# Delta rule steps with a doubled Gram buffer, their preparation moved ahead of the solve

## The chip, the core and the metric

The kernel runs on one core of a Trainium2 chip. The metric is the time on the device of one execution, in microseconds (us), as the median of several runs. The engines are named as in the profile: PE (TensorE matmuls) and PEld (its weight loads), DVE (VectorE), ACT (ScalarE), POOL (GpSimd) and SP (SyncE, which issues most DMAs).

## What is computed

The kernel is a whole two-block network on 256 tokens of width 1024, all in float32. The first block is attention, convolution and memory branches and a mixture of 32 experts. The second block reads the first block's output and a context of 256 tokens; it holds two recurrences, each in two directions: a state space one (SSD) and a gated delta rule (GDN). The change touches the delta rule only. The reference solves it in chunks (cut to what matters):

```python
def gdn_chunk_scan(q, k, v, log_a, beta, s0):
    """Gated delta rule S_t = a_t (I - b_t k_t k_t^T) S_{t-1} + b_t k_t v_t^T, o_t = S_t^T q_t, chunked"""
    g = jnp.cumsum(log_a, axis=2)
    diff = g[:, :, :, None] - g[:, :, None, :]
    a_mat = jnp.einsum("bclhd,bcshd->bclsh", k, k) * beta[:, :, :, None] * masked_exp(diff, strict)
    lhs = jnp.moveaxis(a_mat, -1, 2) + jnp.eye(CHUNK, dtype=a_mat.dtype)
    rhs = jnp.concatenate([v * beta[..., None], k * (beta * jnp.exp(g))[..., None]], -1)
    sol = lax.linalg.triangular_solve(lhs, ..., left_side=True, lower=True, unit_diagonal=True)
    ...
    def step(s, inp):
        v_new = u_c - jnp.einsum("bhlk,bhkv->bhlv", w_c, s)
        o = jnp.einsum("bhlk,bhkv->bhlv", qg_c, s) + jnp.einsum("bhls,bhsv->bhlv", qk_c, v_new)
        s = s * dec_c[..., None, None] + jnp.einsum("bhlk,bhlv->bhkv", kd_c, v_new)
```

## The kernel before, in words

The kernel uses chunks of 128 tokens and 8 heads. There are eight delta steps, m = 0 to 7 (`STEPS`: direction, index in the direction, chunk). Steps 0 to 3 go over the context; they are interleaved with the experts of the first block by a planner (`context_phases` gives each phase a cost, `mixed_schedule` spreads them between the expert phases). Steps 4 to 7 go over the latent tokens and stand behind the experts, with little else beside them.

Every engine runs its own program in order, and waits on semaphores. For the delta steps all four programs (`gdn_pe`, `gdn_act`, `gdn_dve`, `gdn_pool`) walk the same list of phases from `delta_phases`, and each does its own part of a phase. Phases in `STATE_FREE` don't need the state and are done for step m+1 while step m runs. The phases are:

- `rows`: PE turns the cumulated log decays into rows (tile gR), L2058; DVE subtracts and clips them out of PSUM into the matrices A and QK (L1258); ACT takes their exponentials (L1024 for A, L1028 for QK); POOL masks QK (L1624). PE also turns the keys (gkT), which ACT copies out to kT (L1013).
- `gram`: PE forms keys by keys (gKK, L630); DVE multiplies it into A (L1270), copies the diagonal blocks out (L1277, L1279, L1280) and spreads them (L1284).
- `rep`: PE replicates the spread blocks (gRep, L655), ACT copies them to `rep` (L1034); POOL masks A to its off-diagonal part (L1644) and inverts the 16 by 16 diagonal blocks by substitution (L1646, and 15 pairs of L1652 and L1653) into Y.
- `expand`: DVE expands Y to the block diagonal matrix XT (L1294).
- `kS`: PE multiplies keys by the state (gK), ACT scales it into T (L1043), POOL forms U = beta times v (L1633), DVE subtracts T = U - T (L1302).
- `M`, `u`, `M2`, `t`, `w`, `x`, `v`: the block solve. PE multiplies (L630), ACT copies out M, MT, U, M2T and T (L1013), DVE adds the products w, x and v into U (L1305). `M` needs XT. In `M2` POOL also forms k_rest (L1638).
- `cross`: keys by queries (DVE L1290). `out`: the output and the new state (DVE L1316, L1317, L1325, L1326).

PE works into PSUM banks 0 to 5 in turn (`open_tile`: a tile takes the next bank, and PE waits until that bank's last tile is drained). A tile of 4 heads fills a bank, so a phase takes two banks (`M` and `out` up to four). While the experts run, these are banks 0 to 4.

`second_block_pe`, `_act`, `_dve` and `_pool` put other work between the phases of steps 4 to 7: modulation products (PE L2211 and L821, DVE L1469) at the phases of `MOD_PHASES`, and on DVE `q_squares` (L1487) behind `M 4` and `M 5`, on which PE's `q_sums` (L828, behind `M2 4` and `M2 5`) wait; `normed_y` (L1483) behind `kS 6`, `u 6`, `M2 6` and `v 6`; POOL's gate gain (L1709) behind `u 5` and `u 6`.

Steps that use the same chunk as the step before (`SAME_KEYS`: steps 2 and 6) keep its kT.

Of the kernel before, what the change touches and what calls it, by code (L numbers as in the profile page):

```python
# [14 lines left out]
P = 128  # L15
# [6 lines left out]
STATE_FREE = ("rows", "gram", "rep", "cross", "expand")  # L22
# [89 lines left out]
def delta_phases(steps):  # L112

    order = [(phase, steps[0]) for phase in STATE_FREE]
    for m in steps:
        for phase in ("kS", "M", "rows", "u", "M2", "gram", "t", "w", "rep", "x", "v", "cross", "out", "expand"):
            if phase not in STATE_FREE:
                order.append((phase, m))
            elif m + 1 in steps:
                order.append((phase, m + 1))  # L120
    return order


def context_phases():

    delta = {"rows": 2.4, "gram": 2.0, "rep": 3.6, "kS": 1.9, "M": 3.8, "u": 1.9, "M2": 1.9, "t": 1.9, "w": 1.9, "x": 1.9,
# [57 lines left out]
def two_block_kernel(nc, a, out):  # L184
# [3 lines left out]
    with ctx:  # L188
# [26 lines left out]
        AREA = 35760  # L215
        area = sb("area", [P, AREA])

# [144 lines left out]
        def delta_buffers(wide, keys, triangle, MT_at, M2_at, U_at, T_at, K_at, QK_at, small_at):  # L362
            return {"spread": at(wide, 16, GDN_HEADS, 16), "rep": at(wide, 16, GDN_HEADS, 16), "XT": at(wide, GDN_HEADS, P),
                    "kT": at(keys, GDN_HEADS, P), "A": at(triangle, GDN_HEADS, P), "MT": at(MT_at, GDN_HEADS, P),
                    "M2T": at(M2_at, GDN_HEADS, P), "U": at(U_at, GDN_HEADS, P), "T": at(T_at, GDN_HEADS, P),
                    "M": at(K_at, GDN_HEADS, P), "k_rest": at(K_at, GDN_HEADS, P), "QK": [at(place, GDN_HEADS, P) for place in QK_at],
                    "rows": at(small_at, GDN_HEADS, 16), "Y": at(small_at + 128, 16, GDN_HEADS), "step": at(small_at + 256, 16, GDN_HEADS),
                    "pairs": at(small_at + 384, GDN_HEADS, 32)}
# [250 lines left out]
        def gdn_pe(pe, steps, open_tile, transposes):  # L619

            for phase, m in delta_phases(steps):
# [11 lines left out]
                def of(name):  # L633
                    return lambda head: b[name][:, head, :]

                if phase == "rows":
                    pe.wait_ge(s["kn_ready"], c + 1)
                    for h in range(0 if m in SAME_KEYS else 2):
                        transposes(("gkT", m, h), [k_gdn[side][:, t, head * P:(head + 1) * P] for head in range(4 * h, 4 * h + 4)])
                    for h in range(2):  # L640
                        transposes(("gR", m, h), [cum[side][:, d, t, 16 + head:17 + head].to_broadcast([P, P])
                                                  for head in range(4 * h, 4 * h + 4)])
# [93 lines left out]
        def second_block_pe(pe, open_tile, unit, used, transposes, product, tokens_by_weights, split_product):  # L736
# [33 lines left out]
            for i, m in enumerate(LATENT):  # L770
# [19 lines left out]
                if i == 3:  # L790
                    assert next(delta_steps) == "rows 4"
                    gate_tiles(GATES[6:7])
# [211 lines left out]
        def gdn_act(eng, steps):  # L1004

            for phase, m in delta_phases(steps):
# [8 lines left out]
                if phase == "rows":  # L1015
                    for h in range(0 if m in SAME_KEYS else 2):
                        out4("gkT", h, "kT")
                    for h in range(2):
                        part = b["A"][:, 4 * h:4 * h + 4, :]
# [64 lines left out]
        def second_block_act(eng, root, copy_out):  # L1084
# [14 lines left out]
            for i, m in enumerate(LATENT):  # L1099
# [3 lines left out]
                if i == 3:  # L1103
                    assert next(delta_steps) == "rows 4"
                for kind, half, t in GATES[2 * i:2 * i + 2]:
# [134 lines left out]
        def gdn_dve(eng, steps, link, spread):  # L1240

            v = nc.vector
            for phase, m in delta_phases(steps):
# [8 lines left out]
                if phase == "rows":  # L1252
                    for which, clip in (("A", ALU.max), ("QK", ALU.min))[:1 + side]:
                        dst = b["A"] if which == "A" else b["QK"][m % 2]
# [9 lines left out]
                if phase == "gram":  # L1264
                    for h, heads in halves:
                        eng.wait_ge(s["gdn_decay"], 2 * m + h + 1)
                        src = four("gKK", h)
                        for i in range(4):
                            head = 4 * h + i
                            ins = v.scalar_tensor_tensor(b["A"][:, head, :], src[:, i, :], beta[side][:, t, 8 * d + head:8 * d + head + 1],  # L1270
                                                         b["A"][:, head, :], ALU.mult, ALU.mult)
# [3 lines left out]
                    for q in range(4):  # L1275
                        part = slice(32 * q, 32 * q + 32)
                        ins = v.tensor_copy(b["pairs"][part, :, :], b["A"][part, :, part])  # L1277
# [3 lines left out]
                    if m not in (0, 4):  # L1281
                        wait_filled(eng, ("gu", m - 1, 1))
# [96 lines left out]
        def second_block_dve(eng, step, link, root_mean, root_ask, root_take, square_sums, spread):  # L1379
# [27 lines left out]
            for i, m in enumerate(LATENT):  # L1407
# [44 lines left out]
                if i == 3:  # L1452
                    assert next(delta_steps) == "rows 4"
                    assert next(delta_steps) == "gram 4"
# [155 lines left out]
        def gdn_pool(eng, g, steps, link):  # L1610

            for phase, m in delta_phases(steps):
# [27 lines left out]
                if phase == "rep":  # L1640
                    eng.wait_ge(s["spread_ready"], m + 1)
                    for h, heads, dims in halves:
                        part = b["A"][:, heads, :]
# [1250 lines left out]
```

## Time and profile before

| what | value |
|---|---|
| time, median of 3 runs | 1719.59 us (1716.0 to 1723.46) |
| profiled execution: span, first to last instruction | 1712.1 us |
| PE busy | 1554.9 us (91%) |
| PEld busy | 1062.7 us (62%) |
| DVE busy | 693.0 us (40%) |
| ACT busy | 375.5 us (22%) |
| POOL busy | 219.8 us (13%) |
| DMA | 372.53 MB, mean 218 GB/s |
| DMA busy in slices 12 to 22 of 40 | nine tenths or more, but one with seven |

The profiled execution has no time of its own beside its span; the median of the runs is 7.5 us above the span. The chain of work that ended last is PE for 70% of the span, DMA for 16%, DVE for 8%. The page's slices are 42.8 us each: slices 11 to 22 hold the experts and context (DMA at 400 GB/s), slices 29 to 32 the delta steps 4 to 7 (DMA at 50 to 150 GB/s, PE between seven and nine tenths busy). A row of the timeline gives the start, the time from the first to the last of a merged run of instructions, their engine, line, operation, tiles and count, and in brackets how long the engine was idle before it and what ended that.

### The profile page before, as it was taken

The numbers are of one execution on the slowest core, as the hardware profiler recorded it, in microseconds if no ns is written. First come the engines' busy times: TensorE is split into PE (matmuls) and PEld (weight loads), VectorE is DVE, ScalarE is ACT, GpSimd is POOL, SyncE is SP. The second block draws the span as 40 slices with busy tenths as digits, with TensorE's granted clock in tenths as the row PEclk, the third lists the DMA queues.
The fourth block names the chain that finished last, engine by engine and source line by source line (L and its number), as shares of the span: only waits on it lengthen the run. The fifth ranks groups of instructions, "written<-read, shape, count | busy, mean of one in ns | idle before, by whom it ended". The sixth has DMA issues, their size and how long they took to land.

```text
span 1712.1 us, 22993 instructions
## 1 busy us (share of the span) xinstructions
PE 1554.9 (91%) x9392; PEld 1062.7 (62%) x9392; DVE 693.0 (40%) x1459; ACT 375.5 (22%) x829; POOL 219.8 (13%) x368
## 2 busy tenths in 40 slices
PE   7999999999989797888998799999988799999996
PEld 3548655545766464456676478865577764788742
DVE  2206312434533343634443447776766750400003
ACT  1001245201411112232232132142333320100000
POOL 2000000002000000223313010001455512300000
PEclk9999999998999898899999999999999999999998
DMA  8444423564599999799999914442531144344430
GB/s 259 148 147 148 147 98 137 219 227 197 204 407 408 406 408 401 312 399 417 382 373 419 393 64 146 148 145 70 200 140 50 50 148 148 102 160 156 165 130 25
DMA packets 124286, 372.53 MB, mean 218 GB/s; under 512 B 10524, under 2 KB 26518, under 8 KB 107414
## 3 DMA queue, kind: packets, MB, share of 16 engines
q1 hardware_dynamic: 118245, 361.12, 55.8%
q0 software_dynamic: 1568, 8.39, 1.3%
q10 hardware_dynamic: 4368, 1.54, 0.4%
q8 instruction: 77, 1.26, 0.3%
q14 instruction: 28, 0.22, 0.0%
HBM read 369.98 MB, written 1.05 MB: 217 GB/s over the span
## 4 chain that ended last, share of the span: by engine, by line
PE 70%; DMA 16%; DVE 8%; ACT 2%; issue 1%; POOL 1%; SPq 0%; DVEq 0%; ACTq 0%; POOLq 0%
PE psum L2064 48%; PE psum L630 6%; DMA ring<-in_w_down 6%; DMA ring<-in_w_up 5%; PE psum L1859 4%; DMA area<-in_w_in 2%; PE psum L2058 2%; PE psum L1843 2%; PE psum L1900 1%; PE psum L1881 1%; PE psum L655 1%; DMA area<-in_w_down 1%; PE psum L2181 1%; DVE area L1294 1%; POOL area L1652 1%
## 5 line engine op out<-in xcount | busy, mean ns | idle before, releaser
L2064 PE MATMUL psum<-ring,area 128*128 128x512 f32 (+1 forms) x1040 | 448.9, 590 | 8.6 <-DMA ring<-in_w_proj_mem 2.1
L2064 PE MATMUL psum<-area,ring 128*128 128x256 f32 (+1 forms) x1920 | 412.1, 374 | 5.9 <-DMA ring<-in_w_in 4.3
L2064 PEld LDWEIGHTS psum<-area,ring 128*128 128x128 f32 x1920 | 352.8, 191 | 54.3 <-DMA ring<-in_w_in 5.4
L2064 PEld LDWEIGHTS psum<-ring,area 128*128 128x128 f32 x1040 | 196.9, 191 | 246.7 <-issue 243.4
L630 PE MATMUL psum<-area 128*128 128x128 f32 x1536 | 195.3, 286 | 20.7 <-DVE area L1294 17.5
L630 PEld LDWEIGHTS psum<-area 128*128 128x128 f32 x1536 | 185.8, 200 | 43.0 <-issue 19.0
L2337 ACT ACTIVATE area<-psum 128x512 f32<-128x512 f32 x116 | 66.0, 599 | 450.2 <-PE psum L2064 334.0
L1859 PE MATMUL psum<-ring,area 128*32 128x256 f32 x1728 | 111.9, 404 | 34.5 <-DMA ring<-in_w_up 34.4
L1859 PEld LDWEIGHTS psum<-ring,area 128*32 128x32 f32 x1728 | 57.9, 115 | 77.8 <-issue 51.8
L2058 PE MATMUL psum<-const,area 128*128 128x128 f32 x528 | 84.5, 286 | 20.6 <-DVE area L1387 4.8
L2058 PEld LDWEIGHTS psum<-const,area 128*128 128x128 f32 x528 | 65.0, 145 | 55.4 <-issue 24.4
L1210 DVE SCALAR_TENSOR_TENSOR area<-area,cols 128x268 f32<-128x268 f32 (+1 forms) x186 | 91.6, 492 | 6.6
L1601 POOL TENSOR_TENSOR area<-area 128x1024 f32<-128x1024 f32 x4 | 9.8, 2464 | 462.3 <-DVE area L2459 462.3
L1013 ACT COPY area<-psum 128x512 f32<-128x512 f32 x92 | 52.2, 586 | 68.6 <-PE psum L630 63.2
L1881 PE MATMUL psum<-ring,area 128*32 128x256 f32 x800 | 53.7, 399 | 14.4 <-DMA ring<-in_w_down 12.7
L976 ACT COPY area<-psum 128x256 f32<-128x256 f32 x62 | 23.1, 373 | 197.8 <-PE psum L2064 197.8
L1591 DVE TENSOR_TENSOR area<-psum,area 128x512 f32<-128x512 f32 x11 | 7.6, 691 | 140.7 <-PE psum L2064 140.7
L1208 DVE TENSOR_SCALAR area<-area,cols 128x268 f32<-128x268 f32 (+1 forms) x62 | 22.0, 356 | 104.4 <-ACT area L976 104.4
L2064 PE MATMUL psum<-area 128*128 128x256 f32 (+3 forms) x288 | 59.8, 361 | 3.9 <-DMA area<-in_w_in 2.9
L2064 PEld LDWEIGHTS psum<-area 128*128 128x128 f32 (+1 forms) x288 | 47.3, 199 | 14.2 <-issue 5.1
L1551 DVE TENSOR_TENSOR area<-psum,area 128x512 f32<-128x512 f32 x8 | 5.5, 686 | 114.5 <-PE psum L2064 114.5
L1652 POOL TENSOR_TENSOR area<-area 128x120 f32<-128x120 f32 (+14 forms) x120 | 44.9, 374 | 38.7 <-ACT area L1034 29.9
(318 smaller groups left out, 1407.6 us busy)
## 6 DMA issues: line engine op xcount, KB each, us to landing
ring<-in_w_in SPq DMA_DIRECT2D x29, 2048.0 KB, 8.3
ring<-in_w_gate SPq DMA_DIRECT2D x54, 1024.0 KB, 10.2
ring<-in_w_up SPq DMA_DIRECT2D x54, 1024.0 KB, 12.0
ring<-in_w_down SPq DMA_DIRECT2D x50, 1024.0 KB, 13.7
ring<-in_w_ada SPq DMA_DIRECT2D x12, 2048.0 KB, 8.7
area<-in_w_down SPq DMA_DIRECT2D x14, 1024.0 KB, 15.0
ring<-in_w_out SPq DMA_DIRECT2D x6, 2048.0 KB, 7.8
area<-in_w_gate SPq DMA_DIRECT2D x10, 1024.0 KB, 13.1
```

The costliest lines, as they stand in the source:

```text
L630: last = nc.tensor.matmul(dst[:, i * P:(i + 1) * P], lhs(4 * h + i), rhs(4 * h + i), start=True, stop=True)
L976: nc.scalar.copy(dst, src).then_inc(drain_of(key), 1)
L1013: nc.scalar.copy(b[name][:, 4 * h:4 * h + 4, :], src).then_inc(drain_of((key, m, h)), 1)
L1208: link(v.tensor_scalar(dst, src, w, None, ALU.mult))
L1210: link(v.scalar_tensor_tensor(dst, src, w, dst, ALU.mult, ALU.add))
L1652: link(g.tensor_tensor(tmp[:, 0:n, :], rep[:, left, :, j], Y[:, j:j + 1, :].to_broadcast([P, n, GDN_HEADS]), ALU.mult))
L1843: last = nc.tensor.matmul(dst[:, j * P:(j + 1) * P], h2[:, t, k * P:(k + 1) * P], place[:, t, q * P:(q + 1) * P], start=t == 0, stop=t == ...
L1859: last = nc.tensor.matmul(wide.dst[CAP * j:CAP * (j + 1), 0:2 * P], hcT[:, q % 2, k, rows], both[:, :, k % 4, j * P:(j + 1) * P], start=k ...
L1881: last = nc.tensor.matmul(dst[CAP * g:CAP * (g + 1), 0:256], actT_e[:, e % 2, CAP * j:CAP * (j + 1)], w[:, j % 2, g * 256:(g + 1) * 256], ...
L2058: last = nc.tensor.transpose(t[0:width, j * P:j * P + rows], src, ident[0:rows, 0:rows])
L2064: last = nc.tensor.matmul(dst, lhs(k), rhs(k), start=first and k == 0, stop=final and k == count - 1)
L2337: nc.scalar.activation(dst, src, func).then_inc(drain_of(key), 1)
```

## The change

The order of phases in a step becomes

```python
STATE_FREE = ("rows", "keys", "gram", "rep", "cross", "expand")
for phase in ("rows", "kS", "keys", "gram", "M", "u", "M2", "rep", "t", "w", "x", "v", "cross", "out", "expand"):
```

where rows, keys, gram, rep, cross and expand are those of step m+1. Before it was

```python
for phase in ("kS", "M", "rows", "u", "M2", "gram", "t", "w", "rep", "x", "v", "cross", "out", "expand"):
```

The old phase rows is cut in two. On PE, rows keeps the decay rows (gR) and keys has the turned keys (gkT). On ACT everything of it moves to keys: the copies of gkT and the exponentials of A and QK. On DVE the clips stay in rows, and on POOL the mask of QK stays in rows. A gets a second buffer (used by step parity), XT gets one of its own and no longer shares space with spread and rep, and DVE's wait for gu of the step before ahead of the spreading (L1284) is gone. For the space the reserve for descriptors of DMAs that POOL issues is set to 1024 bytes a partition, from its default, and the common area is cut by 300 elements.

```diff
@@ delta_phases, context_phases
-STATE_FREE = ("rows", "gram", "rep", "cross", "expand")
+STATE_FREE = ("rows", "keys", "gram", "rep", "cross", "expand")
...
-        for phase in ("kS", "M", "rows", "u", "M2", "gram", "t", "w", "rep", "x", "v", "cross", "out", "expand"):
+        for phase in ("rows", "kS", "keys", "gram", "M", "u", "M2", "rep", "t", "w", "x", "v", "cross", "out", "expand"):
...
-    delta = {"rows": 2.4, "gram": 2.0, "rep": 3.6, "kS": 1.9, "M": 3.8, "u": 1.9, "M2": 1.9, "t": 1.9, "w": 1.9, "x": 1.9,
+    delta = {"rows": 1.9, "keys": 0.5, "gram": 2.0, "rep": 3.6, "kS": 1.9, "M": 3.8, "u": 1.9, "M2": 1.9, "t": 1.9, "w": 1.9, "x": 1.9,
@@ buffers
-        AREA = 35760
+        AREA = 35460
         area = sb("area", [P, AREA])
+        delta_extra = sb("delta_extra", [P, 2, GDN_HEADS, P])
...
-            return {"spread": at(wide, 16, GDN_HEADS, 16), "rep": at(wide, 16, GDN_HEADS, 16), "XT": at(wide, GDN_HEADS, P),
-                    "kT": at(keys, GDN_HEADS, P), "A": at(triangle, GDN_HEADS, P), "MT": at(MT_at, GDN_HEADS, P),
+            return {"spread": at(wide, 16, GDN_HEADS, 16), "rep": at(wide, 16, GDN_HEADS, 16), "XT": delta_extra[:, 0, :, :],
+                    "kT": at(keys, GDN_HEADS, P), "A": [at(triangle, GDN_HEADS, P), delta_extra[:, 1, :, :]], "MT": at(MT_at, GDN_HEADS, P),
@@ gdn_pe
                 if phase == "rows":
+                    for h in range(2):
+                        transposes(("gR", m, h), [cum[side][:, d, t, 16 + head:17 + head].to_broadcast([P, P])
+                                                  for head in range(4 * h, 4 * h + 4)])
+                if phase == "keys":
                     pe.wait_ge(s["kn_ready"], c + 1)
                     for h in range(0 if m in SAME_KEYS else 2):
                         transposes(("gkT", m, h), [k_gdn[side][:, t, head * P:(head + 1) * P] for head in range(4 * h, 4 * h + 4)])
-                    for h in range(2):
-                        transposes(("gR", m, h), [cum[side][:, d, t, 16 + head:17 + head].to_broadcast([P, P])
-                                                  for head in range(4 * h, 4 * h + 4)])
@@ gdn_act
-                if phase == "rows":
+                if phase == "keys":
                     for h in range(0 if m in SAME_KEYS else 2):
                         out4("gkT", h, "kT")
@@ gdn_dve, phase gram
-                    if m not in (0, 4):
-                        wait_filled(eng, ("gu", m - 1, 1))
                     rows = b["rows"].rearrange("p h j -> p (h j)")
@@ kernel
-    nc = _bacc.Bacc("TRN2", target_bir_lowering=False, num_devices=1)
+    nc = _bacc.Bacc("TRN2", target_bir_lowering=False, num_devices=1, dynamic_dma_scratch_size=1024)
```

Elsewhere b["A"] becomes b["A"][m % 2], and `keys 4` is taken behind `rows 4` in PE's, ACT's and DVE's programs of the second block.

## Rows read from the trace of the kernel before

**Rows 1.** Windows of the expert stage: stretch, length, busy of each engine, clock, DMA share, GB/s
```profile
750.00:765.00 15.00, 15.00 (x156) 9.74 (x155) 5.63 (x14) 8.14 (x14) 0.00 (x0) 1.00 0.93 366
...
810.00:825.00 15.00, 15.00 (x141) 10.89 (x140) 5.82 (x14) 6.47 (x10) 0.00 (x0) 1.00 0.86 340
```
**Rows 2.** Timeline of PE, steps 4 to 6
```profile
1245.03 5.49 PE L630 MATMUL psum<-area 128*128 128x128 f32 x32 [5.89 <-DVE area L1294]
...
1265.16 2.42 PE L655 MATMUL psum<-area,const 128*128 128x512 f32 x8 [1.52 <-DVE area L1284]
1267.42 5.52 PE L630 MATMUL psum<-area 128*128 128x128 f32 x48
...
1286.20 5.39 PE L630 MATMUL psum<-area 128*128 128x128 f32 x32 [3.20 <-DVE area L1294]
...
1295.87 1.84 PE L828 MATMUL psum<-const,area 128*128 128x1 f32 x16
...
1306.69 4.02 PE L655 MATMUL psum<-area,const 128*128 128x128 f32 x8 [3.46 <-DVE area L1284]
1310.55 5.52 PE L630 MATMUL psum<-area 128*128 128x128 f32 x48
...
1349.99 2.42 PE L655 MATMUL psum<-area,const 128*128 128x512 f32 x8 [0.45 <-DVE area L1284]
1352.25 5.52 PE L630 MATMUL psum<-area 128*128 128x128 f32 x48
```
**Rows 3.** Timeline of DVE, the expansion of XT ahead of steps 4, 5, 6, 7
```profile
1241.07 3.90 DVE L1294 TENSOR_TENSOR area<-area,const 128x128 f32<-128x128 f32 x8 [3.53 <-POOL area L1653]
...
1282.79 3.36 DVE L1294 TENSOR_TENSOR area<-area,const 128x128 f32<-128x128 f32 x8
...
1325.90 3.36 DVE L1294 TENSOR_TENSOR area<-area,const 128x128 f32<-128x128 f32 x8
...
1367.32 3.90 DVE L1294 TENSOR_TENSOR area<-area,const 128x128 f32<-128x128 f32 x8 [1.22 <-POOL area L1653]
```
**Rows 4.** Timeline of DVE, its other work in steps 4 to 6
```profile
1244.89 1.28 DVE L1302 TENSOR_TENSOR area<-area 128x512 f32<-128x512 f32 x2
1246.09 0.68 DVE L1469 SCALAR_TENSOR_TENSOR area<-psum,area 128x512 f32<-128x512 f32 x1
1246.69 1.21 DVE L1487 TENSOR_TENSOR area<-area 128x1024 f32<-128x1024 f32 x1
1251.86 4.23 DVE L1258 TENSOR_SCALAR area<-psum,area 128x128 f32<-128x128 f32 x16 [3.96 <-PE psum L2058]
...
1258.63 2.16 DVE L1270 SCALAR_TENSOR_TENSOR area<-psum,area 128x128 f32<-128x128 f32 x8 [0.91 <-PE psum L630]
1260.89 1.18 DVE L1277 COPY area<-area 32x256 f32<-32x256 f32 x4
...
1262.82 2.29 DVE L1284 TENSOR_TENSOR area<-area,stats 128x2048 f32<-128x2048 f32 x1
...
1301.09 2.52 DVE L1277 COPY area<-area 32x256 f32<-32x256 f32 x4
...
1330.38 0.74 DVE L1483 SCALAR_TENSOR_TENSOR area<-area 128x512 f32<-128x512 f32 x1
```
**Rows 5.** Timeline of POOL: mask of QK, first of 30 substitution steps, U
```profile
1255.80 2.50 POOL L1624 TENSOR_TENSOR area<-area,const 128x512 f32<-128x512 f32 x2 [12.72 <-ACT area L1028]
...
1269.21 0.49 POOL L1652 TENSOR_TENSOR area<-area 128x120 f32<-128x120 f32 x1 [1.29 <-ACT area L1034]
...
1282.17 2.08 POOL L1633 TENSOR_TENSOR area<-area 128x512 f32<-128x512 f32 x2
```
**Rows 6.** Windows around M 5; PE's granted clock stands ahead of the DMA share
```profile
1286.20:1288.00 1.80, 1.79 (x8) 1.80 (x9) 1.77 (x4) 0.00 (x0) 0.00 (x0) 0.50 0.00 0
...
1292.00:1296.00 4.00, 4.00 (x39) 4.00 (x38) 3.93 (x16) 3.39 (x5) 0.00 (x1) 1.00 0.00 0
```
**Rows 7.** DMA that POOL issues ahead of rep 4: the page's group of issues
```profile
area<-in_b_ada POOLq DMA_DIRECT2D x1, 2048.0 KB, 12.2
```

More of the change, by code:

```diff
@@ L633, in of @@
                 def of(name):
-                    return lambda head: b[name][:, head, :]
+                    tile = b[name][m % 2] if name == "A" else b[name]
+                    return lambda head: tile[:, head, :]
                 if phase == "rows":
+                    for h in range(2):
+                        transposes(("gR", m, h), [cum[side][:, d, t, 16 + head:17 + head].to_broadcast([P, P])
+                                                  for head in range(4 * h, 4 * h + 4)])
+                if phase == "keys":
                     pe.wait_ge(s["kn_ready"], c + 1)
@@ L791, in second_block_pe @@
                     assert next(delta_steps) == "rows 4"
+                    assert next(delta_steps) == "keys 4"
                     gate_tiles(GATES[6:7])
@@ L1018, in gdn_act @@
                     for h in range(2):
-                        part = b["A"][:, 4 * h:4 * h + 4, :]
+                        part = b["A"][m % 2][:, 4 * h:4 * h + 4, :]
                         if side:
@@ L1104, in second_block_act @@
                     assert next(delta_steps) == "rows 4"
+                    assert next(delta_steps) == "keys 4"
                 for kind, half, t in GATES[2 * i:2 * i + 2]:
@@ L1253, in gdn_dve @@
                     for which, clip in (("A", ALU.max), ("QK", ALU.min))[:1 + side]:
-                        dst = b["A"] if which == "A" else b["QK"][m % 2]
+                        dst = b[which][m % 2]
                         for h, heads in halves:
@@ L1276, in gdn_dve @@
                         part = slice(32 * q, 32 * q + 32)
-                        ins = v.tensor_copy(b["pairs"][part, :, :], b["A"][part, :, part])
+                        ins = v.tensor_copy(b["pairs"][part, :, :], b["A"][m % 2][part, :, part])
                     link(ins)
@@ L1453, in second_block_dve @@
                     assert next(delta_steps) == "rows 4"
+                    assert next(delta_steps) == "keys 4"
                     assert next(delta_steps) == "gram 4"
@@ L1642, in gdn_pool @@
                     for h, heads, dims in halves:
-                        part = b["A"][:, heads, :]
+                        part = b["A"][m % 2][:, heads, :]
                         g.tensor_tensor(part, part, by_row((off_below, off_above)[d]), ALU.mult).then_inc(s["off_ready"], 1)
```

4 lines of the change are left out of this document (2 added, 2 removed).

## The prediction

> **What bounds the kernel now.** I read the page first: its slices split the span into a stage bound by transfers (experts and context, slices 11 to 22) and later ones where PE is busy and DMA isn't. The change touches delta steps 0 to 3 in the first and 4 to 7 in the second. In the windows of the expert stage DMA falls below its full share only where PE is busy all the time [rows 1]; the reader is to see that work of PE which is neither added nor removed, only put elsewhere between experts, has hardly a way to the time there. Then I read the timelines of the engines over steps 4 to 7, 1245 to 1371 us. PE stands still at two places of each step. One is M, for XT: 5.89 us ahead of M 4, 3.20 ahead of M 5 [rows 2]. The other is rep, for DVE's spreading: 1.52, 3.46 and 0.45 us [rows 2]. The expansions of XT end at 1244.97, 1286.15, 1329.26 and 1371.22 [rows 3], so the steps take 41.2, 43.1 and 42.0 us. Step 7 has no step behind it to prepare.
>
> **The change, part by part.** I set each step's clock to 0 at the end of its expansion, and look for the start of x, because all behind it keeps its order. Before, x starts at 1267.42, 1310.55 and 1352.25 [rows 2], thus at 22.5, 24.4 and 23.0.
>
> *PE's queue.* PE now does rows, keys and gram of m+1 ahead of M. In step 4 these lie in the idle 5.89 us [rows 2]. But PSUM has six banks in turn. Counting tiles from cross on: gQK 2, go2 and gS 4; gR takes gQK's banks, gK and gkT the other four, and gKK comes round to gR's. DVE drains gR only by its clips, which stand behind the expansion. So in steps 4 and 6 gKK waits, and in step 5 (no gkT) M itself, for the third and fourth quarter of the 4.23 us of clips [rows 4]: to 3.2 and 4.2. M then ends near 9 to 12, u and M2 near 13 to 16. What decides is whether that is late; it isn't, because of the next part.
>
> *DVE's and POOL's queues.* This is the new wait. POOL's rows (mask of QK for m+1) now stands ahead of its kS (U for m), and the mask waits for ACT's exponentials, these for DVE's clips, these for the expansion. Before, U was made as soon as the substitution was done, at 1282.17 [rows 5], while DVE expanded. Now: clips run 0 to 4.2 [rows 4]; the mask ended at 1258.30, that is 6.4 after the start of the clips at 1251.86 [rows 4, 5]; U takes 2.08 [rows 5], to 8.5; DVE's second subtraction, half of 1.28 [rows 4], ends at 9.2. Behind DVE's subtraction in its queue stands its whole part of gram: 1258.63 to 1265.11, 6.48 us [rows 4]. PE's rep waits for that, and POOL's substitution for rep.
>
> - Step 4: 9.2, plus a modulation of 0.68 [rows 4], plus 6.48, is 16.4. Then comes q_squares, 1.21 [rows 4]: before it stood ahead of gram with nobody waiting, now it is behind, and PE's q_sums stands ahead of rep. 17.6; q_sums 1.84 [rows 2], 19.4; rep 2.42 [rows 2], 21.9. Behind rep now stand t and w, two thirds of 5.52 [rows 2], 3.7. x at 25.5, against 22.5: +3.0.
> - Step 5: 9.2 + 6.48 = 15.7; a short reciprocal (0.2, the gap to a small operation) and q_squares, 17.1; q_sums 18.9; rep 2.42 or, after a wait of over 3 us, 4.02 [rows 2]. PE has had nothing since about 13, so I take 4.02: 22.9; x at 26.6, against 24.4: +2.2.
> - Step 6: 9.2 + 0.74 (normed_y) + 6.48 [rows 4] = 16.4; rep 18.8; x at 22.5, against 23.0: -0.5. There are no q_sums here.
>
> The clock behind the 4.02: after a wait of 3.20 us PE was granted 0.50, the level of 1.2 GHz, against 1.00 (2.4 GHz) a few us later [rows 6].
>
> *The expansions.* U no longer runs beside them. Eight instructions took 3.90 or 3.36 us [rows 3] with U beside them [rows 5]. Without, I take about 2.4, worked from the part of the row behind U: U ended at 1284.25 [rows 5], six instructions remained until 1286.15 [rows 3], so 0.3 each. That gives -0.9, -0.9 and, for step 7, where POOL's substitution also came 1.22 late [rows 3] and now comes earlier (rep ends near 19, copying and substitution take from 1267.58, the end of rep 5, to 1282.17 [rows 2, 5], 14.6, so 33.4; DVE is free at 22.5 + 13.85 = 36.4, the 13.85 from x at 1352.25 to the start of its wait at 1367.32 - 1.22 [rows 2, 3]), -1.2 for the wait and -0.8 for an expansion that U, now released by the output's matmuls, still overlaps in part: together -3.8.
>
> *Collisions.* POOL's U for the second half runs when DVE could subtract the first half. If DVE is held until 8.5, as at the expansions, each step is 0.6 later: +1.9 for three. POOL's k_rest and gate gain fall on DVE's small copies of gram in step 5, which cost 2.52 instead of 1.18 [rows 4]: +1.3. The mask of A starts as q_squares does in step 5: between 0 and half its 2.50 (the like mask [rows 5]), I take 0.6. In step 4 k_rest can reach the spreading: 0 to 1, I take 0.3. Sum +4.1, bounds 0 and 5.4.
>
> The Trainium skill, page "SBUF — State Buffer", section "Who interferes with whom", says that a DVE instruction with two inputs in SBUF contends with GpSimd instructions that read SBUF, and not one with a PSUM input. The expansions beside U agree with it. By it the clips are safe and the subtraction is not; if it didn't hold, the sum would lack the 1.9.
>
> *Sum for steps 4 to 7*: 3.0 + 2.2 - 0.5 - 3.8 + 4.1 = +5.0. Against the profiled execution that is 1712.1 + 5.0 = 1717.1 of span; its own surroundings put the median 7.5 above the span, so 1719.6 + 5.0 = 1724.6. Bounds: no collision and no low clock in step 5, -0.7; everything at the upper end, with the low clock in step 4 too (+1.6) and expansions not faster (+2.4), near +10.
>
> *Steps 0 to 3.* The planner puts the same phases between the experts; the total cost grows by 0.5 for keys 0. Wait of PE on others is rare there, and the last phases, from kS 3 on, keep their places. I take 0. From both sides: in [rows 1] DMA lost 7% and 14% of 15 us, 3.2 us in two stretches, in which experts' gathering and scattering meet M and solve phases, and there are about two more such; a better or worse fall of the phases is worth about 6 us either way, at most.
>
> *Descriptor reserve.* It concerns only the copies that POOL issues: three on end ahead of the context, two ahead of rep 4, four behind step 7. They don't depend on it if their descriptors fit. No row shows the reserve's use; taken at 0, with the other end in rival 2.
>
> *Removed wait and separate buffers.* DVE's wait for gu has no row as a wait; the removal itself is 0, and only permits the order.
>
> **The rivals.**
>
> 1. *Faster: U comes in time.* If kS on POOL doesn't hold DVE, subtraction ends at 5.5, gram at 12.0 (plus 0.68 or 0.74), and PE is the limit: rep at about 15.8, 15.2 and 14.3 (M2 ends at 14, 13.4 and 14.3, behind it q_sums of 1.84 [rows 2] in the first two), and with rep 2.42 and 3.7 for t and w x at 21.9, 21.3 and 20.4: -0.6, -3.1 and -2.6, with the expansions' -3.8: -10.1, 1709.5. For it: before, U was ready before the subtraction in every step. Against: the order of POOL's phases in the code, and DVE's last clip must precede.
> 2. *Slower: the reserve is too small.* If POOL must wait ahead of rep 4 until its 2048 KB copy has landed, 12.2 us [rows 7], instead of the about 1 us that issuing takes, the mask and substitution of rep 4 start 11 us later, and DVE already waits for them (3.53 [rows 3]): +11 on the path to M 4, on top of the forecast 1735.6. It decides from the point at which the descriptors of two copies don't fit. The Trainium skill, page "DMA: Bandwidth & Descriptors", section "SWDGE vs HWDGE vs iDMA", places these rings in that reserve, and gives no rule by which these copies overflow it.
> 3. *Slower: upper ends together*, low clock after each wait of PE for spreading, all collisions: +10, 1729.6.
> 4. *Experts' stage fills or opens DMA holes*: 6 us either way on top of the forecast: 1718.6 or 1730.6.
> 5. *The change does nothing*: PE's idle time only moves from M and rep to gram and rep with the same length; 1719.6. It lies in the forecast's range.
>
> **How the numbers follow.** Forecast with rival 5: 0.64, own range 1717 to 1729. Rival 1: 0.08. Rival 2: 0.06. Rival 3: 0.09. Rival 4: 0.05 down, 0.08 up. A measurement of this kernel can tell about 0.5%, 8.6 us, from no change: 1711 and 1728.2 are the limits. Faster takes rival 1 and little else: 0.09. Slower takes rivals 2, 3 and the upper 4 and a tail of the forecast: 0.26. Same: 0.65. The range 1713 to 1733 leaves out rival 1's middle and the worst of rival 2.
>
> **What would show it.** In the profile after: POOL L1624 ahead of L1633 in each step, and DVE L1302 waiting for POOL L1633, by 3 us or more; the expansions near 2.4 us; PE L630 of gram or M waiting for DVE L1258; the start of x at about 26, 27 and 23 us behind the expansion; L828 waiting for DVE L1487 in steps 4 and 5. If DVE does not wait at L1302, rival 1 is right. If POOL stands at L1700 or L1702, rival 2 is. If the experts' stage ends at another time, rival 4 is.

## The result and the profile after

The changed kernel takes 1735.75 us (median of 4 runs, 1731.12 to 1742.52), the kernel before 1719.34 in the 4 runs beside it (1716.00 to 1723.46). The ratio is 1.0099, with a 95% interval of 1.0067 to 1.013: about 17 us slower, between 11.5 and 22. The forecast was 1724.6 with a range from 1713 to 1733. The ratios here and below leave out three executions far above the rest (5561.53 us of e1_reserve, 1750.33 of e8_context_old_fixed, and 2288.95 of the kernel before beside e5 to e8), which the medians include.

| | before | after |
|---|---|---|
| profiled execution: span | 1712.1 | 1734.0 |
| start of the experts' last scatter on PE | 974.1 | 983.9 |
| its end | 977.8 | 990.4 |
| end of the expansion ahead of step 4 | 1245.0 | 1255.8 |
| steps 4, 5, 6, between the ends of their expansions | 41.2, 43.1, 42.0 | 48.4, 46.0, 41.4 |
| from the end of the expansion ahead of step 7 to the end | 340.9 | 342.4 |
| PE, DVE, POOL busy | 1554.9, 693.0, 219.8 | 1563.8, 691.3, 225.1 |

The two spans are 21.9 us apart, the medians 16.4. The profiled execution of after has a time of its own, 1735.84, which is 1.8 above its span. Before's span is 7.5 below its median. If its surroundings were 1.8 too, then most of that was a short execution, and the spans overstate the loss by some 5 us.

The time is lost in two places. In these two executions the experts' stage loses some 10 us, steps 4 to 6 lose 7.2 + 2.9 - 0.6 = 9.5, and 1.5 come behind them.

**The experts' stage.** Timeline of PE in the changed kernel, two stretches (columns as in [rows 2]):

```profile
804.59 1.07 PE L1885 MATMUL psum<-ring,area 128*32 128x256 f32 x16 [1.05 <-DMA ring<-in_w_down]
...
805.76 3.74 PE L1847 MATMUL psum<-area 128*128 128x128 f32 x32
809.33 1.95 PE L631 MATMUL psum<-area 128*128 128x128 f32 x16
811.12 2.74 PE L1904 MATMUL psum<-area 128*128 128x512 f32 x6
817.63 1.13 PE L1904 MATMUL psum<-area 128*128 128x512 f32 x2 [3.77 <-DVE x L2007]
818.59 5.36 PE L631 MATMUL psum<-delta_extra 128*128 128x128 f32 x32
823.88 3.66 PE L1863 MATMUL psum<-ring,area 128*32 128x256 f32 x64
...
875.46 1.93 PE L1885 MATMUL psum<-ring,area 128*32 128x256 f32 x32
...
891.59 1.93 PE L1863 MATMUL psum<-ring,area 128*32 128x256 f32 x32
```

Only L1863 (gate and up) and L1885 (down) read `ring`, where the experts' weights land. Between the last down, which ends at 805.66, and the next gate, at 823.88, 18.2 us pass with other things: gather (L1847), gram, scatter (L1904), a wait, M. In that time PE frees no buffer of weights. From 877.39 to 891.59 it is 14.2 us, of which 0.5 is a wait. Before, the same stretches were 806.46 to 818.11, 11.7, and 872.83 to 883.56, 10.7:

```profile
805.39 1.07 PE L1881 MATMUL psum<-ring,area 128*32 128x256 f32 x16 [1.36 <-DMA ring<-in_w_down]
...
818.11 1.93 PE L1859 MATMUL psum<-ring,area 128*32 128x256 f32 x32
...
870.90 1.93 PE L1881 MATMUL psum<-ring,area 128*32 128x256 f32 x32
...
883.56 1.93 PE L1859 MATMUL psum<-ring,area 128*32 128x256 f32 x32
```

The first stretch hardly grew by more work. PE stands still for 3.77 us in it, and then M takes 5.36 us, where the 32 matmuls of M took 3.74 before, at 806.56. The clock over M was 0.67. These two are 5.4 of the 6.5 us by which the stretch grew. In the second stretch most of the growth is work: gram and M lie in it, where the decay rows (gR) and u lay before.

```profile
818.60:823.80 5.20, 5.20 (x33) 5.16 (x31) 0.86 (x2) 1.76 (x3) 0.00 (x0) 0.67 0.03 9
```

Windows of the changed kernel over and behind these stretches (columns as in [rows 1]: the share of DMA is next to last, ahead of it the clock):

```profile
810.00:825.00 15.00, 11.23 (x75) 8.42 (x76) 9.01 (x20) 2.75 (x5) 0.00 (x0) 0.89 0.53 213
885.00:900.00 15.00, 15.00 (x149) 10.45 (x152) 6.40 (x9) 6.25 (x10) 1.46 (x2) 1.00 0.57 220
```

and of the kernel before over the second of them:

```profile
885.00:900.00 15.00, 14.68 (x189) 10.90 (x184) 8.65 (x20) 4.79 (x9) 4.79 (x5) 1.00 0.88 344
```

DMA's share falls to 0.53 where it was 0.86 [rows 1], and to 0.57 where it was 0.88. That is (0.86 - 0.53) x 15 + (0.88 - 0.57) x 15 = 9.6 us of transfers in a stage that is bound by them. The two stretches grew by 6.5 and 3.5, 10.0 together, and the last scatter starts 9.7 us later. That the three agree so well is in part luck: e1_reserve (below), which has the code of before in this stage, starts its last scatter 6.1 us later than before does. The four kernels with the old order here (before, e1, e2, e8) start it at 971.5 to 980.2, 974.4 in the mean, the four with the new order (after, e3, e4, e5) at 979.0 to 987.4, 982.4 in the mean, 8.0 later. The wait of 3.77 us ahead of L1904 has its cause on DVE: the additions of the scatter stand behind a whole gram.

```profile
810.49 2.16 DVE L1275 SCALAR_TENSOR_TENSOR area<-psum,area 128x128 f32<-128x128 f32 x8 [0.20 <-PE psum L631]
...
814.68 2.29 DVE L1287 TENSOR_TENSOR area<-area,stats 128x2048 f32<-128x2048 f32 x1
816.89 2.67 DVE L2007 TENSOR_TENSOR x<-psum,x 128x512 f32<-128x512 f32 x4
```

**Steps 4 to 6.** Timeline of DVE in the changed kernel:

```profile
1253.40 2.40 DVE L1297 TENSOR_TENSOR delta_extra<-area,const 128x128 f32<-128x128 f32 x8 [3.52 <-POOL area L1657]
...
1263.24 2.06 DVE L1305 TENSOR_TENSOR area<-area 128x512 f32<-128x512 f32 x2 [3.30 <-POOL area L1637]
...
1270.00 2.29 DVE L1287 TENSOR_TENSOR area<-area,stats 128x2048 f32<-128x2048 f32 x1
1272.21 2.06 DVE L1491 TENSOR_TENSOR area<-area 128x1024 f32<-128x1024 f32 x1
...
1301.76 2.42 DVE L1297 TENSOR_TENSOR delta_extra<-area,const 128x128 f32<-128x128 f32 x8
...
1311.63 4.19 DVE L1305 TENSOR_TENSOR area<-area 128x512 f32<-128x512 f32 x2 [3.31 <-POOL area L1637]
...
1357.66 4.20 DVE L1305 TENSOR_TENSOR area<-area 128x512 f32<-128x512 f32 x2 [3.31 <-POOL area L1637]
```

POOL and PE in step 4:

```profile
1259.65 2.49 POOL L1628 TENSOR_TENSOR area<-area,const 128x512 f32<-128x512 f32 x2 [6.28 <-ACT area L1032]
1262.10 2.04 POOL L1637 TENSOR_TENSOR area<-area 128x512 f32<-128x512 f32 x2
```

```profile
1259.05 3.75 PE L631 MATMUL psum<-area 128*128 128x128 f32 x16 [5.85 <-DVE area L1263]
...
1274.32 3.58 PE L832 MATMUL psum<-const,area 128*128 128x1 f32 x16 [3.29 <-DVE area L1491]
1277.76 4.61 PE L658 MATMUL psum<-area,const 128*128 128x512 f32 x8
1282.16 9.82 PE L631 MATMUL psum<-area 128*128 128x128 f32 x80
```

The new wait is there. POOL's mask (L1628) waits for ACT, U (L1637) stands behind it, and DVE stands still for 3.3 us at the subtraction (L1305) in each of the three steps. Behind the subtraction are gram and q_squares (L1491), behind these PE's q_sums (L832), and behind them rep (L658). In step 4 both q_sums and rep run at half the clock, as windows show, behind a wait of 3.29 us (the clock is the third number from the end):

```profile
1274.40:1277.70 3.30, 3.30 (x16) 3.30 (x17) 0.00 (x0) 0.00 (x0) 3.30 (x4) 0.50 0.00 0
1277.80:1282.00 4.20, 4.20 (x9) 2.38 (x10) 0.17 (x1) 0.00 (x0) 0.04 (x1) 0.50 0.00 0
```

0.50 is the level of 1.2 GHz. Before, q_sums of step 5 took 1.84 and rep of step 4 took 2.42 [rows 2]; q_sums of step 4 took 1.84 too.

### The profile page after: what moved, and what is told of

Its sections match the earlier page's. It is cut to its first block, busy times and chain, and to the rows that moved or that the text cites. A ratio compares the mean times of both kernels' runs of the same rounds, so it can differ in the third digit from the quotient of the medians.

```text
span 1734.0 us, 22986 instructions
## 1 busy us (share of the span) xinstructions
PE 1563.8 (90%) x9392; PEld 1070.0 (62%) x9392; DVE 691.3 (40%) x1459; ACT 376.0 (22%) x829; POOL 225.1 (13%) x368
## 4 chain that ended last, share of the span: by engine, by line
PE 68%; DMA 18%; DVE 8%; ACT 2%; issue 2%; POOL 1%; SPq 0%; DVEq 0%; ACTq 0%; POOLq 0%
PE psum L2068 48%; DMA ring<-in_w_down 8%; PE psum L631 5%; DMA ring<-in_w_up 5%; PE psum L1863 3%; DMA area<-in_w_in 2%; PE psum L2062 2%; PE psum L1847 2%; PE psum L1904 2%; PE psum L1885 1%; PE psum L2215 1%; DMA area<-in_w_down 1%; PE psum L2185 1%; PE psum L658 1%; PE psum L612 1%
## 5 line engine op out<-in xcount | busy, mean ns | idle before, releaser
L631 PE MATMUL psum<-area 128*128 128x128 f32 x1152 | 145.7, 284 | 11.1 <-DVE area L1263 9.5
L631 PEld LDWEIGHTS psum<-area 128*128 128x128 f32 x1152 | 138.0, 197 | 28.4 <-issue 24.2
L1863 PE MATMUL psum<-ring,area 128*32 128x256 f32 x1728 | 111.2, 402 | 37.1 <-DMA ring<-in_w_up 36.8
L1863 PEld LDWEIGHTS psum<-ring,area 128*32 128x32 f32 x1728 | 58.5, 115 | 79.7 <-issue 54.7
L1885 PE MATMUL psum<-ring,area 128*32 128x256 f32 x800 | 53.4, 393 | 18.6 <-DMA ring<-in_w_down 17.9
L1595 DVE TENSOR_TENSOR area<-psum,area 128x512 f32<-128x512 f32 x11 | 7.6, 692 | 142.2 <-PE psum L2068 142.2
L1213 DVE TENSOR_SCALAR area<-area,cols 128x268 f32<-128x268 f32 (+1 forms) x62 | 22.1, 356 | 104.6 <-ACT area L980 104.6
L2018 DVE TENSOR_TENSOR area<-psum,area 128x128 f32<-128x128 f32 x32 | 9.3, 290 | 114.2 <-ACT area L1970 112.5
L1308 DVE TENSOR_TENSOR area<-area,psum 128x512 f32<-128x512 f32 x48 | 32.9, 688 | 50.6 <-PE psum L631 50.3
## 6 DMA issues: line engine op xcount, KB each, us to landing
ring<-in_w_gate SPq DMA_DIRECT2D x54, 1024.0 KB, 10.4
```

What stands on the lines that cost most here:

```text
L631: last = nc.tensor.matmul(dst[:, i * P:(i + 1) * P], lhs(4 * h + i), rhs(4 * h + i), start=True, stop=True)
L1308: v.tensor_tensor(b["U"][:, heads, :], b["U"][:, heads, :], four(key, h), sign).then_inc(drain_of((key, m, h)), 1)
L1863: last = nc.tensor.matmul(wide.dst[CAP * j:CAP * (j + 1), 0:2 * P], hcT[:, q % 2, k, rows], both[:, :, k % 4, j * P:(j + 1) * P], start=k ...
L1885: last = nc.tensor.matmul(dst[CAP * g:CAP * (g + 1), 0:256], actT_e[:, e % 2, CAP * j:CAP * (j + 1)], w[:, j % 2, g * 256:(g + 1) * 256], ...
```

## The experiments

All of them compute the whole network. Each ratio is to runs of the kernel before on the same chip in the same job, with a 95% interval. The landmarks are from one profiled execution each, and totals vary between executions: the 28 runs of before beside the first four experiments reach from 1711.5 to 1727.6. Ratios carry the verdicts on totals; the landmarks say where the time is. A loss or gain in us that is given from a ratio is that share of 1719.

| kernel | median | ratio | last scatter starts | steps 4, 5, 6 |
|---|---|---|---|---|
| before | 1719.34 | 1 | 974.1 | 41.2, 43.1, 42.0 |
| after | 1735.75 | 1.0099 (1.0067 to 1.013) | 983.9 | 48.4, 46.0, 41.4 |
| e1_reserve | 1722.73 | 1.0002 (0.9979 to 1.0026) | 980.2 | 41.4, 43.0, 42.2 |
| e2_context_old | 1726.39 | 1.0033 (1.001 to 1.0057) | 971.8 | 47.8, 45.4, 41.4 |
| e3_latent_old | 1731.52 | 1.0046 (1.0027 to 1.0065) | 987.4 | 41.8, 44.1, 42.8 |
| e4_mask_later | 1730.99 | 1.0062 (1.0034 to 1.009) | 979.4 | 46.3, 45.6, 39.1 |
| e5_mask_sums | 1720.87 | 1.0007 (0.9994 to 1.0021) | 979.0 | 41.0, 40.5, 39.1 |
| e6_plan | 1720.99 | 1.001 (0.9993 to 1.0027) | 976.5 | 48.7, 49.4, 41.4 |
| e7_before_plan | 1708.34 | 0.9931 (0.9904 to 0.9959) | 969.8 | 41.2, 43.1, 42.2 |
| e8_context_old_fixed | 1716.60 | 0.9977 (0.9955 to 0.9998) | 971.5 | 41.0, 40.5, 39.2 |
| e9_all | 1704.33 | 0.9906 (0.9886 to 0.9925) | 964.0 | 41.6, 40.5, 39.1 |
| e10_new_order_all | 1707.53 | 0.9934 (0.9912 to 0.9957) | 969.4 | 41.0, 40.5, 39.1 |
| e11_mask_held | 1704.13 | 0.9906 (0.9891 to 0.992) | 968.8 | 40.5, 41.5, 37.2 |

### The parts of the change by themselves

**e1_reserve**: the kernel before with the smaller reserve alone.

```diff
-    nc = _bacc.Bacc("TRN2", target_bir_lowering=False, num_devices=1)
+    nc = _bacc.Bacc("TRN2", target_bir_lowering=False, num_devices=1, dynamic_dma_scratch_size=1024)
```

> The kernel before with nothing changed but the reserve for descriptors (1024 bytes a partition). Theory A (the loss is the order of the phases): no change, within 3 us of before. Rival R (the smaller reserve holds up POOL's copies or the transfers of the experts' stage): 5 to 17 us slower, with POOL idle at its copies or the experts' stage ending later than at 982 us.

Measured: 1.0002. The smaller reserve costs nothing that can be told, and the rival in which POOL waits for its descriptors is refuted.

**e2_context_old**: the changed kernel with the old order in steps 0 to 3 (`keys` directly behind `rows`).

```diff
-        for phase in ("rows", "kS", "keys", "gram", "M", "u", "M2", "rep", "t", "w", "x", "v", "cross", "out", "expand"):
+        for phase in (("kS", "M", "rows", "keys", "u", "M2", "gram", "t", "w", "rep", "x", "v", "cross", "out", "expand") if m < 4 else
+                      ("rows", "kS", "keys", "gram", "M", "u", "M2", "rep", "t", "w", "x", "v", "cross", "out", "expand")):
```

> The changed kernel, with the old order of phases for steps 0 to 3 and the new one for steps 4 to 7; buffers and reserve as changed. Theory A (9 us are lost in the experts' stage because the new order puts M and gram of steps 1 and 2 between the gathering and scattering of the experts, 8 us in steps 4 to 7): 8 us slower than before; the last scatter starts as in before (974 us, within 3), steps 4 to 6 take 48, 46 and 41 us. Rival R (buffers or reserve): the experts' stage stays 9 us longer and the total is 17 us over before.

**e3_latent_old**: the other half, the new order for m < 4 and the old one for steps 4 to 7.

```diff
-        for phase in ("rows", "kS", "keys", "gram", "M", "u", "M2", "rep", "t", "w", "x", "v", "cross", "out", "expand"):
+        for phase in (("rows", "kS", "keys", "gram", "M", "u", "M2", "rep", "t", "w", "x", "v", "cross", "out", "expand") if m < 4 else
+                      ("kS", "M", "rows", "keys", "u", "M2", "gram", "t", "w", "rep", "x", "v", "cross", "out", "expand")):
```

> The changed kernel, with the new order for steps 0 to 3 and the old one for steps 4 to 7. Theory A: 9 us slower than before, all of it before 985 us; steps 4 to 6 take about 41, 42 and 41 us, since the separate buffer for XT and the missing wait change nothing there. Rival (buffers' places slow the steps 4 to 7): 17 us slower.

Measured: e2 is 0.33% slower than before (5.7 us) and e3 0.46% (7.9 us); their sum, 13.6, lies in the interval of the whole change. In e2 the last scatter starts 2.4 us earlier than before and steps 4 to 6 cost 8.3 more; in e3 the scatter starts 13.3 us later and the steps cost 2.4 more. So both halves of the loss are real, and each comes from the order in its own stage. Their sizes are less sure: the intervals are 1.7 to 9.8 us for e2 and 4.6 to 11.2 for e3, and the medians of e3 alone would give 12.1.

### The wait in steps 4 to 6

**e4_mask_later**: POOL's mask moves from `rows` to `keys`, that is behind U.

```diff
@@ gdn_pool
-                if phase == "rows" and side:
+                if phase == "keys" and side:
                     for h, heads, dims in halves:
                         part = b["QK"][m % 2][:, heads, :]
@@ second_block_pool
             assert next(delta_steps) == "rows 4"
+            assert next(delta_steps) == "keys 4"
```

> The changed kernel with POOL's mask of QK moved from phase rows to phase keys, so behind its U of phase kS. Theory A: DVE's wait of 3.3 us for POOL ahead of the subtraction goes in each of steps 4 to 6, so these three steps get 6 to 9 us shorter together, and the kernel is 7 to 10 us slower than before instead of 17. Rival C (steps 4 to 6 are bound by PE's wait for the clips and its low clock behind it): under 2 us of change against the changed kernel.

Measured: 0.62% slower than before. DVE's wait for U is gone, but the steps are only 4.7 us shorter than after's (131.1 instead of 135.8), less than expected, and the kernel is 10.7 us above before, where 7 to 10 were expected. Timelines of DVE and PE in e4:

```profile
1256.89 3.28 DVE L1305 TENSOR_TENSOR area<-area 128x512 f32<-128x512 f32 x2
...
1267.07 2.06 DVE L1491 TENSOR_TENSOR area<-area 128x1024 f32<-128x1024 f32 x1
```

```profile
1269.19 2.87 PE L832 MATMUL psum<-const,area 128*128 128x1 f32 x16 [2.19 <-DVE area L1491]
1271.92 4.61 PE L658 MATMUL psum<-area,const 128*128 128x512 f32 x8
```

The subtraction takes 3.28 instead of 1.28 [rows 4]: now the mask runs beside it. And PE still waits for q_squares, behind which q_sums and rep run slowly.

**e5_mask_sums**: e4 and, besides, q_sums behind w instead of M2 (in PE's and DVE's programs), so that rep no longer stands behind them.

```diff
-                if phase in ("M2 4", "M2 5"):
+                if phase in ("w 4", "w 5"):
                     q_sums(int(phase[-1]) - 4)
```

> The kernel of e4 (mask of QK behind U) with PE's q_sums and DVE's reading of them moved from behind M2 4 and M2 5 to behind w 4 and w 5, so behind rep. If rep waits for q_squares and q_sums in steps 4 and 5: 46.3 and 45.6 us become 41 to 42, step 6 stays at 39.2, and the three are 4 us shorter than before's 126.3; the total is 4 to 6 us above before, what is left being the experts' stage. If PE's bank wait for the clips binds instead: no change against e4.

Measured: no difference from before (1.0007, which is 1.2 us, between 1.0 less and 3.6 more), where 4 to 6 us above it were expected. The three steps take 120.6, 5.6 less than before and 15.2 less than after; by the ratios the total is 15.8 less than after's. PE in e5:

```profile
1266.81 2.42 PE L658 MATMUL psum<-area,const 128*128 128x512 f32 x8 [0.17 <-DVE area L1287]
...
1273.12 1.84 PE L832 MATMUL psum<-const,area 128*128 128x1 f32 x16
```

rep waits 0.17 and takes 2.42; q_sums take 1.84. So the wait for U and the place of q_sums are the whole loss of these steps and more. The new order is better here once the two queues follow it. That the total is level all the same leaves some 7 us (1.2 + 5.6) for the experts' stage, which agrees with e3.

### The experts' stage

**e6_plan**: the changed kernel, with a planner that places no phase of the context, delta steps and others, directly behind a gather or a scatter, nor behind the turns of experts 13, 17, 21 and 25. This is where the 18.2 us piled up and part of the 14.2: ahead of turn 25, behind down 24, keys 3 and gram 3 still find a place.

```diff
@@ mixed_schedule
         order.append(("expert", phase))
+        e = phase.split()[-1]
+        if phase.startswith(("gather", "scatter")) or (phase.startswith("turn") and int(e) % 4 == 1 and 12 < int(e) < 28):
+            continue
```

> The changed kernel, with the planner taking no context phase between turn 17, 21, 25, the gathering and the scattering; they come behind the next gate product. Theory A (the experts' stage loses because context phases pile up where PE frees no weights): the last scatter starts 6 to 10 us earlier than in the changed kernel (at 980 to 984 instead of 990), total 7 to 11 us above before. Rival D (it is DVE's gram block ahead of the scatter's additions alone): the loss stays, since gram 2 still stands near.

**e7_before_plan**: the same edit on the kernel before.

> The kernel before with the same restriction of the planner. Theory A: where DMA stood at 86 to 93% it comes near its full share, 2 to 6 us faster than before. If before lost nothing to the piling up: within 2 us of before.

Measured: e6 is level with before (1.001), 15 us below after, where 7 to 11 above before were expected; e7 is 0.69% faster than before, 11.9 us by the ratio and 9.8 by the medians, with four runs, and more than expected. PE and windows in e7:

```profile
801.28 1.07 PE L1884 MATMUL psum<-ring,area 128*32 128x256 f32 x16 [1.36 <-DMA ring<-in_w_down]
802.45 3.74 PE L1846 MATMUL psum<-area 128*128 128x128 f32 x32
806.02 3.60 PE L1903 MATMUL psum<-area 128*128 128x512 f32 x8
809.55 1.93 PE L1862 MATMUL psum<-ring,area 128*32 128x256 f32 x32
```

```profile
805.00:825.00 20.00, 20.00 (x200) 14.79 (x199) 6.84 (x17) 9.27 (x16) 2.04 (x2) 1.00 0.93 373
865.00:885.00 20.00, 20.00 (x200) 14.79 (x200) 6.46 (x15) 9.86 (x17) 2.04 (x2) 1.00 0.93 374
```

The same two windows of the kernel before:

```profile
805.00:825.00 20.00, 19.61 (x187) 14.92 (x188) 6.66 (x16) 9.19 (x15) 0.00 (x0) 1.00 0.90 360
865.00:885.00 20.00, 19.73 (x197) 15.40 (x201) 7.71 (x18) 9.24 (x19) 0.00 (x0) 1.00 0.93 379
```

From the last down to the next gate it is 7.2 us instead of 11.7, but DMA's share, 0.93 in both places, is hardly above that of before, 0.90 and 0.93. The last scatter starts 4.3 us earlier than before's and 10.4 earlier than e1's. So that the placing is worth about 12 us is shown by the total, since e7 has nothing else; how it comes about is not shown by its trace. The restriction also moves work at other places. For one, 18.8 us without a read of `ring` that begin at 673.0 in before become stretches of 9.9 and 6.4. e6 gained more than its profile accounts for: its profiled execution took 1726.93, the longest of its runs, with steps 4 to 6 at 139.4 us. How much of its 15 us undoes the new order and how much is the gain that e7 has too isn't settled by it. Nor does it part PE's work from DVE's gram ahead of the scatter (rival D), since it moves gram 2 and M 1 out of the stretch together: both now come behind the next gate.

### Together

**e8_context_old_fixed**: e5 with the old order in steps 0 to 3, as in e2. **e9_all**: e8 with the edit of e6. **e10_new_order_all**: e5 with the edit of e6, so the new order everywhere.

> The kernel of e5 with the old order of phases for steps 0 to 3. Experts' stage as before, steps 4 to 6 as in e5: 3 to 5 us faster than before.

> Old order for steps 0 to 3, the planner's restriction of e7, new order with mask and q_sums moved (as e8) for steps 4 to 7. If the two effects are separate and add: 10 us (e7) plus 4 us (e8), 14 us faster than before, experts' last scatter near 973, steps 41.0, 40.5, 39.2.

> The same with the new order for steps 0 to 3 as well (the kernel of e5 with the planner's restriction). Theory A: the order itself costs nothing in the experts' stage once the phases don't pile up at the gathering; last scatter within 4 us of e9, total within 4 us of e9. If the new order costs by itself (DVE's gram block ahead of the experts' work): 5 us or more slower than e9.

Measured: 0.9977, 0.9906 and 0.9934. e9 is 16 us faster than before (15 by the medians) and fits the sum of its parts, e7's 11.9 and e8's 4.0, each by its ratio. e8's interval, 0.3 to 7.7 us, only just leaves out no change. e10 is 3.2 us above e9 by the medians and 4.8 by the ratios, its last scatter starts 5.4 later, and the intervals allow both nothing and 10 us: between the two theories it isn't decided. The same step from old order to new, without the restriction, is 5.2 us (e5 against e8, by the ratios), so the restriction cannot be said to cure it. The trace of e10 shows why some loss may stay: one long stretch is left, 864.2 to 877.2, 13.0 us where e9 has 7.2. PE waits in it behind DVE's gram of step 3.

```profile
862.01 2.22 PE L1889 MATMUL psum<-ring,area 128*32 128x256 f32 x32
...
875.30 1.98 PE L1908 MATMUL psum<-area 128*128 128x512 f32 x4 [2.09 <-DVE area L1951]
877.21 1.93 PE L1867 MATMUL psum<-ring,area 128*32 128x256 f32 x32
```

DMA's share from 860 to 880 is 0.83 in e10 and 0.97 in e9.

**e11_mask_held**: e9, with POOL's mask moved to phase u and held there until DVE's subtraction is done.

```diff
@@ gdn_pool, on e9
-                if phase == "keys" and side:
-                    for h, heads, dims in halves:
+                def masked_qk(m):
...
+                if phase == "rows" and m == 4:
+                    masked_qk(4)
+                if phase == "u" and 4 <= m < 7:
+                    eng.wait_ge(s["r_ready"], 2 * (m - 2) + 2)
+                    masked_qk(m + 1)
```

> The kernel of e9 with POOL's mask of QK held back until DVE has subtracted (behind U, in phase u). If the 3.28 us of the two subtractions (1.28 before) come from POOL's mask running beside them: they take 1.3 us, rep waits less, steps 4 to 6 shorter by 0.3 to 1.5 us each, total 1 to 4 us faster than e9. If the 3.28 us have another cause: no change.

DVE of e9, steps 4 and 5:

```profile
1241.49 3.27 DVE L1309 TENSOR_TENSOR area<-area 128x512 f32<-128x512 f32 x2
...
1283.07 3.29 DVE L1309 TENSOR_TENSOR area<-area 128x512 f32<-128x512 f32 x2
...
1288.54 1.18 DVE L1286 COPY area<-area 32x256 f32<-32x256 f32 x4
```

and of e11:

```profile
1246.01 1.27 DVE L1309 TENSOR_TENSOR area<-area 128x512 f32<-128x512 f32 x2
...
1286.56 1.28 DVE L1309 TENSOR_TENSOR area<-area 128x512 f32<-128x512 f32 x2
...
1290.01 3.52 DVE L1286 COPY area<-area 32x256 f32<-32x256 f32 x4
```

The mechanism is confirmed: the same subtraction takes 3.27 beside the mask and 1.27 without. The gain hardly is. Steps 4 to 6 take 119.2 in the profiled execution instead of 121.2, and the medians are level (1704.13 and 1704.33); 2 us are less than the intervals can tell. In step 4 it saves 1.1 and in step 6 2.0. In step 5 it loses 1.0, because POOL's work now falls on the small copies of gram, which take 3.52 instead of 1.18, as [rows 4] had shown of step 5 with 2.52. The collision was moved, not removed.

## Why the prediction was wrong

**Steps 0 to 3: the step that failed.** The prediction said "I take 0", and that a better or worse fall of the phases is worth "about 6 us either way, at most". e3 measures 7.9 us (4.6 to 11.2). The reason for the 0 was that moved work of PE "has hardly a way to the time there", and that PE's wait on others is rare. [rows 1] was priced by the holes that DMA already had (3.2 us in two stretches), and not by how deep one gets when the time between two reads of `ring` grows by half. That time was in the timeline of before, 11.7 us. In the changed kernel a wait of PE for DVE, 3.77 us, and the lower clock behind it are more than half of what the two stretches grew by, and DMA stands at 0.53 while PE is busy for only 11.23 of 15 us. The order of phases is worked out by the planner before anything runs, so it could have been listed: between turn 21 and the next gate it was M 1, gather 6, scatter 4, rows 2, and became keys 2, gather 6, gram 2, scatter 4, M 1. By the planner's costs that is 6.2 and 6.3, the same; what it doesn't price is that DVE's gram now stands ahead of DVE's part of the scatter. No run parts that wait from the placing of PE's work. The direction stood as rival 4, at 0.08 and with 6 us.

**Steps 4 to 6: right in mechanism, too small.** The forecast gave +3.0, +3.8 and -1.9 (its +3.0, +2.2 and -0.5 with the expansions and the collisions); it was +7.2, +2.9 and -0.6. That is 9.5 instead of 5.0 in the profiled execution, and 8.3 in that of e2; e2's total gives 5.7 (1.7 to 9.8) for this half. So the steps are mis-sized by 3 to 5 us in the traces, while the total alone would not have shown it. In us behind the end of the expansion, the chain of step 4 (the forecast without its 0.9 for collisions):

| | forecast | measured |
|---|---|---|
| U ends | 8.5 | 8.3 |
| subtraction ends | 9.2 | 9.5 |
| gram ends | 16.4 | 16.5 |
| q_squares end | 17.6 | 18.5 |
| q_sums end | 19.4 | 22.1 |
| rep ends | 21.9 | 26.6 |
| x starts | 25.5 | 30.3 |

The start of x is that of the merged row at 1282.16 and 32 of its 80 matmuls, 3.9 us, for t and w. PE's waits for the clips (5.85, 2.73 and 3.65 us) and DVE's wait of 3.3 were where the forecast put them. PE also waited 0.66, 4.27 and 2.88 us for DVE's product of gram (L1275), which the forecast had not; rep, which waits for the whole of gram, was held up by that 0.2 us at most. In step 4 two terms were mis-sized. The low clock was a term in step 5 (4.02 for rep) and only an upper end of 1.6 in step 4. It came in step 4, on q_sums (3.58 instead of 1.84) and on rep (4.61 instead of 2.42), together 3.9, and not in step 5, where rep took 2.40 and the wait ahead of q_sums was 1.79. And q_squares take 2.06 instead of 1.21 in step 4, beside POOL's k_rest (1270.22 to 1275.16), which the forecast had put at 0.3 on the spreading.

In steps 5 and 6 the mis-sized term is the subtraction: 4.2 us, so that it ends at 11.6, where the forecast had 9.2 and a collision of 0.6. What runs beside its second part is POOL's gate gain (1312.47 to 1315.28 in step 5). The forecast had put that on the small copies of gram, at 1.3, and these took 1.18, with POOL idle beside them. The low clock that was put on rep of step 5, 1.6 too much, made up for part of it. x starts at 28.2 and 25.1 instead of 26.6 and 22.5.

**The expansions: right.** About 2.4 was forecast ahead of steps 5 and 6, 2.42 and 2.43 measured. Ahead of step 7 it was 3.1, for an overlap with U in part, and 2.43 measured; the wait of 1.22 is gone, as forecast. In e4 and e5, where U runs beside the first part of the expansion ahead of step 4, it takes 3.9 as before.

**Collisions.** The prediction weighed the rule of the Trainium skill, page "SBUF — State Buffer", section "Who interferes with whom": a DVE instruction with two inputs in SBUF contends with GpSimd instructions that read SBUF. The runs agree, with 1.27 us alone against 3.27 beside the mask. The clips, which the rule calls safe, took 2.15 for eight in every step, but POOL was idle beside nearly all of them, so they test nothing. A test of that side is DVE's product of gram, with one input in PSUM: 2.16 beside POOL's gate gain in step 5 of before, 2.15 with POOL idle in step 5 of after.

**Surroundings.** Adding the forecast +5.0 to the median was right; to call the 7.5 between span and median "surroundings" was not. After's own are 1.8, as in every execution that has both numbers (1.7 to 1.9).

**Rivals.** Rival 1 (U in time) is refuted by the waits of 3.30 and 3.31, rival 2 (the reserve) by e1, rival 5 (nothing changes) by the ratio. Rival 3, the upper ends together, came close in the profiled execution, +9.5 instead of +10, but not by its own terms: the low clock fell on rep and q_sums of step 4 only, and most of the rest was the subtraction beside the gate gain. The result is rivals 3 and 4 at once, up to 10 for the one and about 8 for the other; the range let only one of them happen at a time. Two unknown costs in different stages add up, and the range should have reached 1719.6 + 10 + 6 = 1735.6 even by the prediction's own numbers.

## What to carry to other kernels

When phases are put elsewhere between work bound by transfers, list the new order and look for the longest stretch in which the engine that frees the buffers frees none. Here such stretches grew by 10.0 us, by work and by waits for another engine's queue, and DMA lost 9.6 us in them. When an order is changed for one engine, walk every other engine's queue by it: here a mask of 2.5 us ahead of U and sums ahead of rep turned a gain of 5.6 us in three steps into a loss of 9.5. Add the bad ends of independent stages before the range is set.

## What was not expected of the hardware

Two subtractions of 128x512 on DVE with both inputs in SBUF take 1.27 us alone and 3.27 beside POOL's mask of 2.49. In e4 the mask ran from 1256.68 to 1259.62 and the subtractions from 1256.89 to 1260.17, 3.5 us for both, where one after the other is 1.27 + 2.49 = 3.8: the overlap is worth 0.3. In steps 5 and 6 of after, where POOL's gate gain of 2.80 runs beside the second of them, they take 4.20.

The experts' last scatter took 3.67 us in some profiled executions (before, e1, e2, e6, e7) and 5.27 to 6.64 in others (after, e3, e4, e5, e8 to e11). The clock there was 1.00 in before and 0.52 in after. PE had stood still for 1.5 us ahead of it in both, and in the two stops before that for 1.48 and 0.53 us in before, for 1.28 and 1.65 in after. Which it is doesn't follow the change, since e9, one of the fastest, had the longest. What decides it stays open.
